# Storing the high and low parts of a matmul's moving operand in alternating pieces of 32 tokens

## The chip, the cores and the metric

The kernel runs on one core of a Trainium2 chip. The metric is the device time of one launch in microseconds. 256 columns are 256 tokens throughout.

## The reference

Two transformer blocks work on 256 latent tokens of 1024 channels. The first block normalizes and modulates the tokens, projects them, mixes them (window attention with a sink beside a two-way mLSTM), projects again and applies a SwiGLU. The second block (with 16 meta tokens ahead, 272 in all) has a SwiGLU, a mixer of attention and gated linear attention with a gate per branch, and a second SwiGLU. What matters here is the dense part, nearly all of the work:

```python
def swiglu(h, w_in, w_out):
    gate, up = jnp.split(h @ w_in, 2, axis=-1)
    return (jax.nn.silu(gate) * up) @ w_out
```

Everything is float32. There are three such SwiGLUs, with an inner width of 2816, and between them the input, output, branch and gate projections.

## The kernel before

Activations lie with channels on the 128 partitions and tokens along the free axis, so a dense layer is a chain of matmuls whose stationary operand is a 128x128 block of weights and whose moving operand is one channel block (k) of all tokens. To keep float32 accuracy on the fp32r path, weights and activations are both split into a high and a low part, and every product is three matmuls into one PSUM bank: high weights by high tokens, high weights by low tokens, low weights by high tokens (`split_mm`, L2003 to L2007; the same three, written out, at L2398 for the first output projection).

Weights stream through a ring of four slots: SP's queue loads `raw`, ScalarE copies it to `hi` (L621), VectorE makes `lo` as raw minus hi (L1143), TensorE multiplies. Each matmul has a weight load of its own, which the trace shows as an instruction of its own (PEld).

The token operands are kept in three pairs of buffers:

- `mixH` and `mixL`, [128, 8, 256] each, one behind the other. They hold the mixed tokens of the first block (L2398), the two branches of the second mixer (`branch_part`), and the normalized input of the last SwiGLU (`gu2`).
- `g_high` and `g_low`, the inner activations of the SwiGLUs, read by `down_half`; 256 tokens wide in `dn0` and `dn2`, 272 wide in `dn1`.
- `n_high` and `n_low`, the normalized tokens of all other dense stages, 258, 272 or 256 columns wide. The change leaves them alone.

The stages follow each other in this order on TensorE: input projections, attention and mLSTM, `wout`, `gu0`, `dn0`, `gu1`, `dn1`, `in2k`, `in2g` with the second mixer in between, `brb`, `bra`, `wout2`, `gu2`, `dn2`. `gu` is the gate and up projection, `dn` the down projection. The order is written out by hand; nothing in it depends on a planner. The first stages of `stage`, a buffer for parts of the modulation's weights that GpSimd's queue loads, share their memory with `mixH` and `mixL`.

Of the kernel before, what the change touches and what calls it, by code (L numbers as in the profile page):

```python
# [28 lines left out]
SLOT = HALF * P  # L29
RING = 4  # L30
# [84 lines left out]
def program(nc, dr, out):  # L115
    with ExitStack() as root:
# [27 lines left out]
        mixH = sbuf(root, "mixH", [P, KD, T], F32R)  # L144
        mixL = sbuf(root, "mixL", [P, KD, T], F32R)
# [224 lines left out]
        def inner(store, width):  # L370

            return store[:, 0:KH * width].rearrange("p (k t) -> p k t", k=KH)
# [132 lines left out]
        def _(pool):  # L505
# [12 lines left out]
            def stage_half(n, freed=0):  # L518
# [87 lines left out]
        def _(act):  # L606
# [193 lines left out]
            def heads_out(n, hp):  # L800
# [4 lines left out]
                act.activation(mixH[:, hp, :], head_bank(n), ACT.Copy).then_inc(oh_ready, 1)  # L805
# [98 lines left out]
            for h in range(4):  # L904
# [3 lines left out]
                act.activation(mixH[:, 4 + h, :], HT_BANK[h], ACT.Copy,  # L908
# [16 lines left out]
            def gate_up_shifted(name, ahead):  # L925
                def evac(i, j):
# [6 lines left out]
                    if j == 3:  # L933

                        act.wait_ge(hb_ready, i + 1)
                        act.activation(inner(g_high, T)[:, ds(2 * i, 2), :], hbuf[:, :, 0:T], ACT.Copy).then_inc(gh_ready, 1)
                pipeline(name, 1024, evac, ahead, silu=True, behind=((0,), (1,), (), (2, 3)), shifted=True)

            def gate_up_scaled(name, f, width, ahead):
                def evac(i, j):  # L940
# [4 lines left out]
                    if j == 3:  # L945

                        act.wait_ge(acc_free[1], USE[name] + i + 1)
                        act.activation(inner(g_high, width)[:, ds(2 * i, 2), :], hbuf[:, :, 0:width], ACT.Copy).then_inc(gh_ready, 1)
# [5 lines left out]
            def upper(scale, k, width, t0, updated, to=nH):  # L954

                act.wait_ge(*updated)
                act.activation(to[:, k, 0:width], R[:, k, t0:t0 + width], ACT.Copy, scale=scale).then_inc(nh_ready, 1)
# [124 lines left out]
            for n in range(8):  # L1082
# [11 lines left out]
                if n in LINEAR_AT:  # L1094
                    i = LINEAR_AT[n]
                    act.wait_ge(yb_ready, i + 1)
                    act.activation(mixH[:, 4 + i:8:2, :], og[:, 2 * i:2 * i + 2, 0:T], ACT.Copy).then_inc(ybh_ready, 1)
# [32 lines left out]
        def _(dve):  # L1130
# [57 lines left out]
            def col(c):  # L1188
                return vec[:, c:c + 1]
# [120 lines left out]
            def modulation(n):  # L1310
# [4 lines left out]
                for b in range(2):  # L1315
                    m, w = 16 + 2 * n + b, stage[:, 2 * b + 1 - side, :]
# [105 lines left out]
            def heads_lower(n, hp):  # L1422

                dve.wait_ge(oh_ready, n + 1)
                dve.tensor_tensor(mixL[:, hp, :], head_bank(n), mixH[:, hp, :].bitcast(F32),
# [151 lines left out]
            for h in range(4):  # L1577
                dve.wait_ge(mlh_ready, h + 1 if h < 2 else 4)
                dve.scalar_tensor_tensor(out=mixL[:, 4 + h, :], in0=HT_BANK[h], scalar=col(V_GML + h),
                                         in1=mixH[:, 4 + h, :].bitcast(F32), op0=ALU.mult, op1=ALU.subtract).then_inc(mll_ready, 1)  # L1580
# [63 lines left out]
            def scaled_lower(first, k, width, t0, scale, to=(nH, nL)):  # L1644

                dve.wait_ge(nh_ready, first + k + 1)
                dve.scalar_tensor_tensor(out=to[1][:, k, 0:width], in0=R[:, k, t0:t0 + width],
# [1147 lines left out]
```

## Time and profile before

| | |
|---|---|
| Median of 3 runs | 971.9 us (969.46 to 973.7) |
| The profiled execution's own time | 973.39 us, its span 971.6 us |
| TensorE busy | 956.6 us, 98% of the span |
| Weight loads busy | 888.0 us, 91% |
| VectorE, ScalarE, GpSimd busy | 641.1, 495.0, 66.6 us |
| Mean granted TensorE clock | 0.994 |

A matmul's duration in the trace (some 280 ns at 256 columns) is longer than the step from one matmul's start to the next one's, since they are pipelined. What the stream costs is the step. It is read from a row that gives the first and last start of the matmuls of one source line: with n matmuls on that line, and two of the other two lines between each two, the step is (last start minus first start) / (3 (n - 1)).

### The profile page before, as it was taken

The page shows a single profiled execution, that of the slowest core. Times are in us where ns is not written, and L with a number is a line of the kernel's source. Part 1 is how long each engine was busy: PE and PEld are TensorE (multiplying, and loading weights), DVE is VectorE, ACT ScalarE, POOL GpSimd, SP SyncE. Part 2 cuts the span into 40 slices and gives each one's busy share as a digit, 9 for nine tenths or more (in the row PEclk, how much of TensorE's full clock was granted, in tenths as well). Part 3 has the DMA queues.
Part 4 walks back from the last instruction along what each step waited for, and adds up shares of the span by engine and source line. Part 5 has one row for each costly group of instructions (what it writes and reads, how often), then busy time and mean ns, then how long its engine had stood idle before and what let it go on. Part 6 is the DMA issues. An engine that isn't in the chain of part 4 may idle for free.

```text
span 971.6 us, 19403 instructions
## 1 busy us (share of the span) xinstructions
PE 956.6 (98%) x7543; PEld 888.0 (91%) x7543; DVE 641.1 (66%) x990; ACT 495.0 (51%) x762; POOL 66.6 (7%) x100
## 2 busy tenths in 40 slices
PE   8999999999999999999999999999999999999997
PEld 3776778899999999899999999999999999999997
DVE  4788886687666765765555546665778766665654
ACT  3755647655444544554444434645566555444540
POOL 0012002200000021000000000200210100000000
PEclk9999998999999999999999999999999999999999
DMA  9982447547556696266666844663445566667841
GB/s 346 384 283 88 131 131 231 163 172 216 173 174 182 191 308 177 71 197 173 176 177 183 217 119 129 212 188 108 131 131 173 154 194 204 184 177 220 217 120 43
DMA packets 189183, 176.06 MB, mean 181 GB/s; under 512 B 7312, under 2 KB 177824, under 8 KB 188752
## 3 DMA queue, kind: packets, MB, share of 16 engines
q1 hardware_dynamic: 183456, 154.29, 53.9%
q0 software_dynamic: 4960, 17.64, 5.3%
q10 hardware_dynamic: 720, 3.49, 0.9%
q8 instruction: 31, 0.51, 0.2%
q14 instruction: 16, 0.13, 0.0%
HBM read 174.32 MB, written 1.05 MB: 180 GB/s over the span
## 4 chain that ended last, share of the span: by engine, by line
PE 87%; DVE 8%; ACT 2%; issue 1%; DMA 1%; POOL 0%; DVEq 0%; ACTq 0%; POOLq 0%
PE acc L2005 23%; PE acc L2006 23%; PE acc L2007 23%; PE acc L2398 3%; DVE lo L1143 2%; PE acc L2101 1%; DMA stage<-in_w_late 1%; PE acc L2203 1%; PE acc L2205 1%; PE acc L2204 1%; PE wk L2064 1%; PE wk L2005 1%; PE wk L2006 1%; PE wk L2007 1%; PE wk L2134 1%
## 5 line engine op out<-in xcount | busy, mean ns | idle before, releaser
L1143 DVE TENSOR_TENSOR lo<-raw,hi 128x1024 fp32r<-128x1024 f32 (+1 forms) x259 | 331.5, 1291 | 208.0 <-ACT hi L621 207.7
L621 ACT ACTIVATE hi<-raw 128x1024 fp32r<-128x1024 f32 (+1 forms) x260 | 283.8, 1099 | 133.5 <-PE acc L2007 114.7
L2005 PE MATMUL acc<-n_high,hi 128*128 128x272 f32 (+3 forms) x1016 | 290.5, 286 | 0.5 <-DVE hbuf L1671 0.3
L2006 PE MATMUL acc<-n_low,hi 128*128 128x272 f32 (+3 forms) x1016 | 289.2, 285 | 0.0
L2007 PE MATMUL acc<-n_high,lo 128*128 128x272 f32 (+3 forms) x1016 | 288.1, 284 | 0.0
L2005 PEld LDWEIGHTS acc<-n_high,hi 128*128 128x128 f32 (+1 forms) x1016 | 191.4, 188 | 3.1 <-issue 1.4
L2006 PEld LDWEIGHTS acc<-n_low,hi 128*128 128x128 f32 (+1 forms) x1016 | 191.0, 188 | 0.5
L2007 PEld LDWEIGHTS acc<-n_high,lo 128*128 128x128 f32 (+1 forms) x1016 | 191.0, 188 | 0.2
L2005 PE MATMUL acc<-g_high,hi 128*128 128x256 f32 (+1 forms) x528 | 148.9, 282 | 0.9 <-DVE lo L1143 0.9
L2006 PE MATMUL acc<-g_low,hi 128*128 128x256 f32 (+1 forms) x528 | 149.1, 282 | 0.0
L2007 PE MATMUL acc<-g_high,lo 128*128 128x256 f32 (+1 forms) x528 | 148.7, 282 | 0.0
L2005 PE MATMUL acc<-mixH,hi 128*128 128x256 f32 x400 | 112.9, 282 | 0.5 <-DVE gab L1844 0.4
L2006 PE MATMUL acc<-mixL,hi 128*128 128x256 f32 x400 | 112.1, 280 | 0.0
L2007 PE MATMUL acc<-mixH,lo 128*128 128x256 f32 x400 | 112.1, 280 | 0.0
L2005 PEld LDWEIGHTS acc<-g_high,hi 128*128 128x128 f32 x528 | 99.3, 188 | 1.2 <-DVE lo L1143 1.1
L2007 PEld LDWEIGHTS acc<-g_high,lo 128*128 128x128 f32 x528 | 99.9, 189 | 0.0
L2006 PEld LDWEIGHTS acc<-g_low,hi 128*128 128x128 f32 x528 | 99.1, 188 | 0.0
L2006 PEld LDWEIGHTS acc<-mixL,hi 128*128 128x128 f32 x400 | 76.5, 191 | 0.0
L2005 PEld LDWEIGHTS acc<-mixH,hi 128*128 128x128 f32 x400 | 75.1, 188 | 1.5 <-DVE gab L1844 0.7
L2007 PEld LDWEIGHTS acc<-mixH,lo 128*128 128x128 f32 x400 | 75.1, 188 | 0.0
L566 POOL TENSOR_TENSOR sq<-sq 128x256 f32<-128x256 f32 (+1 forms) x28 | 23.8, 851 | 482.7 <-ACT sq L923 431.0
L923 ACT ACTIVATE sq<-R (+3 forms) x36 | 15.9, 441 | 57.6 <-DVE R L1715 49.9
(424 smaller groups left out, 1254.5 us busy)
## 6 DMA issues: line engine op xcount, KB each, us to landing
raw<-in_w_in SPq DMA_DIRECT2D x52, 512.0 KB, 3.8
raw<-in_w_ffn_in SPq DMA_DIRECT2D x44, 512.0 KB, 3.9
raw<-in_ffn_w_gate SPq DMA_DIRECT2D x44, 512.0 KB, 3.9
raw<-in_ffn_w_up SPq DMA_DIRECT2D x44, 512.0 KB, 3.8
raw<-in_ffn_w_down SPq DMA_DIRECT2D x32, 704.0 KB, 4.8
stage<-in_w_late POOLq DMA_DIRECT2D x24, 512.0 KB, 5.4
raw<-in_w_ffn_out SPq DMA_DIRECT2D x16, 704.0 KB, 6.2
raw<-in_w_out SPq DMA_DIRECT2D x16, 512.0 KB, 3.6
```

Source lines behind the costliest of these rows:

```text
L566: ins = pool.tensor_tensor(sq[:, 0, 0:width], sq[:, 0, 0:width], sq[:, k, 0:width], ALU.add)
L621: act.activation(hi[:, j, 0:width], raw[:, j, 0:width], ACT.Copy).then_inc(hi_ready, 1)
L923: act.activation(sq[:, k, 0:width], R[:, k, t0:t0 + width], ACT.Square).then_inc(sq_ready, 1)
L1143: dve.tensor_tensor(lo[:, j, 0:width], raw[:, j, 0:width], hi[:, j, 0:width].bitcast(F32), ALU.subtract).then_inc(lo_ready, 1)
L2005: pe.matmul(out_, wH, xH, start=start, stop=False)
L2006: pe.matmul(out_, wH, xL, start=False, stop=False)
L2007: return pe.matmul(out_, wL, xH, start=False, stop=stop)
L2064: ins = pe.matmul(SLAB_BANK[n][32 * kk:32 * kk + 32, :], silu_c[:, 4 * q + kk, :], SLAB_MEM[n][2 * q + kk // 2][:, 512 * (kk % 2):512 * (k ...
L2101: pe.matmul(acc[:, 0, 0:width], cink[:, 0, 0, 0:P], cink.rearrange("p a b t -> p (a b t)")[:, 0:width], start=True, stop=True)
L2134: ins = pe.matmul(bank[:, T * m:T * m + T], ws[:, j, w], xs[:, k, 0:T], start=k == 0 and m == 0 and n == 0, stop=k == KD - 1 and n == 2, s ...
L2203: pe.matmul(out_, n5H[:, k, rows], hi[:, k // 2, w], start=k == 0, stop=False)
L2398: ins = pe.matmul(out_, ws[:, j, w], xs[:, k, :], start=k == 0 and m == 0 and n == 0, stop=k == KD - 1 and n == 2, skip_group_check=True)
```

## The change

The two parts of the mixed tokens share one buffer, `mix`, in which 32 tokens of the high part (128 bytes) are followed by the same 32 tokens of the low part, and so on. The two parts of the inner activations do the same in `inner` where the width is 256; at 272, which isn't a multiple of 32, they still lie one behind the other, without the 32 elements of padding that stood between them. So the moving operand of the matmuls that read them has eight pieces of 32 columns with 128 bytes left out between two, and covers 2 KB where it covered 1 KB. ScalarE and VectorE write the same pieces. `stage` takes its slots in another order, so that the same halves of the channel blocks come free at the same time. The order and number of instructions stay as they were on every engine, and so do all other buffers' places.

```diff
-        mixH = sbuf(root, "mixH", [P, KD, T], F32R)
-        mixL = sbuf(root, "mixL", [P, KD, T], F32R)
+        mix = sbuf(root, "mix", [P, KD, T // PIECE, 2, PIECE], F32R)
+        mixH, mixL = mix[:, :, :, 0, :], mix[:, :, :, 1, :]
...
-        g_high = sbuf(ffn2, "g_high", [P, KH * TM], F32R)
+        inner = sbuf(ffn2, "inner", [P, 2 * KH * TM], F32R)
         sbuf(ffn2, "pad_h", [P, 32])
-        g_low = sbuf(ffn2, "g_low", [P, KH * TM], F32R)
...
+        def inner_parts(width):
+
+            if width == T:
+                g = inner[:, 0:2 * KH * T].rearrange("p (k g h c) -> p k g h c", k=KH, h=2, c=PIECE)
+                return g[:, :, :, 0, :], g[:, :, :, 1, :]
+            return tuple(inner[:, n * KH * width:(n + 1) * KH * width].rearrange("p (k t) -> p k t", k=KH) for n in range(2))
...
-                    pool.dma_start(stage[:, 2 * b + 1 - side, :],
+                    pool.dma_start(stage[:, 2 - 2 * side + b, :],
...
-                act.activation(mixH[:, hp, :], head_bank(n), ACT.Copy).then_inc(oh_ready, 1)
+                act.activation(mixH[:, hp], in_pieces(head_bank(n)), ACT.Copy).then_inc(oh_ready, 1)
...
-                        dve.tensor_tensor(inner(g_low, width)[:, ds(2 * i, 2), :], hbuf[:, :, 0:width],
-                                          inner(g_high, width)[:, ds(2 * i, 2), :].bitcast(F32),
+                        high, low = (n[:, ds(2 * i, 2)] for n in inner_parts(width))
+                        dve.tensor_tensor(low, shaped_as(hbuf[:, :, 0:width], low), high.bitcast(F32),
                                           ALU.subtract).then_inc(gl_ready, 1)
...
-            def split_mm(out_, wH, wL, xH, xL, start, stop):
-
+            def split_mm(out_, j, w, xH, xL, start, stop):
+
+                out_, wH, wL = shaped_as(out_, xH), hi[:, j, w], lo[:, j, w]
                 pe.matmul(out_, wH, xH, start=start, stop=False)
                 pe.matmul(out_, wH, xL, start=False, stop=False)
                 return pe.matmul(out_, wL, xH, start=False, stop=stop)
```

## Rows read from the trace of the kernel before

**Rows 1.** The page: busy time of each engine, the granted clock in 40 slices.

```profile
PE 956.6 (98%) x7543; PEld 888.0 (91%) x7543; DVE 641.1 (66%) x990; ACT 495.0 (51%) x762; POOL 66.6 (7%) x100
...
PEclk9999998999999999999999999999999999999999
```

**Rows 2.** The page: the chain that ended last.

```profile
PE 87%; DVE 8%; ACT 2%; issue 1%; DMA 1%; POOL 0%; DVEq 0%; ACTq 0%; POOLq 0%
```

**Rows 3.** TensorE's waits: line waited for, us in total, times, longest.

```profile
PE acc L2101 <- POOL cink L508: 2.5, 1, 2.5
PE wk L2005 <- DVE n_low L1647: 1.7, 4, 0.8
PE acc L2005 <- DVE lo L1143: 0.9, 1, 0.9
```

**Rows 4.** Groups of TensorE by form, of the matmuls that the change touches.

```profile
L2005 PE MATMUL acc<-mixH,hi 128*128 128x256 f32 x400 | 112.9, 282 | 0.5 <-DVE gab L1844 0.4
...
L2005 PE MATMUL acc<-g_high,hi 128*128 128x256 f32 x352 | 98.2, 279 | 0.9 <-DVE lo L1143 0.9
...
L2398 PE MATMUL acc<-mixH,hi 128*128 128x256 f32 x64 | 19.3, 301 | 0.0
...
L2005 PE MATMUL wk<-mixH,hi 128*128 128x256 f32 x16 | 4.4, 276 | 0.0
```

**Rows 5.** Line L2006 in parts of dn0, gu2, dn2: min/median/max ns, first and last start.

```profile
L2006 PEld LDWEIGHTS acc<-g_low,hi x118: 187/188/188, 344.9 to 384.7; 128*128 128x128 f32 x118
L2006 PE MATMUL acc<-g_low,hi x118: 276/276/276, 345.1 to 384.8; 128*128 128x256 f32 x118
...
L2006 PEld LDWEIGHTS acc<-mixL,hi x270: 192/192/192, 799.9 to 895.0; 128*128 128x128 f32 x135
L2006 PE MATMUL acc<-mixL,hi x269: 281/281/281, 800.0 to 894.7; 128*128 128x256 f32 x135
...
L2006 PE MATMUL acc<-g_low,hi x142: 281/281/281, 905.1 to 954.9; 128*128 128x256 f32 x142
```

**Rows 6.** The same line at 258 columns (gu0), 272 columns (gu1) and 272 columns (dn1).

```profile
L2006 PE MATMUL acc<-n_low,hi x238: 277/283/294, 232.1 to 318.0; 128*128 128x258 f32 x119
...
L2006 PE MATMUL acc<-n_low,hi x254: 287/288/296, 429.8 to 524.7; 128*128 128x272 f32 x127
...
L2006 PE MATMUL acc<-g_low,hi x157: 287/291/292, 534.8 to 593.7; 128*128 128x272 f32 x157
```

**Rows 7.** TensorE in order of time around the first pass of gu2.

```profile
782.38 0.28 PE L2005 MATMUL wk<-mixH,hi 128*128 128x256 f32 x1
782.50 0.28 PE L2006 MATMUL wk<-mixL,hi 128*128 128x256 f32 x1
782.61 0.28 PE L2007 MATMUL wk<-mixH,lo 128*128 128x256 f32 x1
782.73 0.59 PE L2051 MATMUL wk<-sq,cst 128*128 128x256 f32 x2
783.16 1.03 PE L2055 MATMUL wk<-sq,cst 128*128 128x256 f32 x4
```

**Rows 8.** Stretches: PE, PEld, DVE, ACT, POOL busy, granted clock, DMA share, GB/s.

```profile
345.00:385.00 40.00, 40.00 (x355) 40.00 (x355) 24.72 (x24) 17.84 (x23) 8.18 (x8) 1.00 0.85 247
800.00:895.00 95.00, 95.00 (x809) 95.00 (x808) 58.22 (x61) 44.94 (x59) 0.00 (x0) 1.00 0.69 199
```

**Rows 9.** ScalarE and VectorE groups that write the two parts.

```profile
L948 ACT ACTIVATE g_high<-hbuf 128x512 f32 x9 | 5.7, 632 | 18.2 <-DVE hbuf L1671 18.2
...
L1674 DVE TENSOR_TENSOR g_low<-hbuf,g_high 128x512 f32 x9 | 6.2, 693 | 8.6 <-ACT g_high L948 8.6
...
L1647 DVE SCALAR_TENSOR_TENSOR mixL<-R,vec,mixH 128x256 fp32r<-128x256 f32 x8 | 4.2, 568 | 1.4 <-ACT mixH L957 1.4
```

More of the change, by code:

```diff
@@ L29 @@
 SLOT = HALF * P
+PIECE = 32
 RING = 4
@@ L368, in keys_to, with in_pieces, shaped_as, pieces @@
             return META + P * (b + 1)
-        def inner(store, width):
-            return store[:, 0:KH * width].rearrange("p (k t) -> p k t", k=KH)
+        def in_pieces(a):
+            return a.rearrange("p (g c) -> p g c" if len(a.shape) == 2 else "p k (g c) -> p k g c", c=PIECE)
+        def shaped_as(a, other):
+            return in_pieces(a) if len(other.shape) > len(a.shape) else a
+        def pieces(s):
+            return slice(s.start // PIECE, s.stop // PIECE)
+        def inner_parts(width):
[3 more added lines that the diff above has]
+            return tuple(inner[:, n * KH * width:(n + 1) * KH * width].rearrange("p (k t) -> p k t", k=KH) for n in range(2))
         def chunk(c):
@@ L947, in evac @@
                         act.wait_ge(acc_free[1], USE[name] + i + 1)
-                        act.activation(inner(g_high, width)[:, ds(2 * i, 2), :], hbuf[:, :, 0:width], ACT.Copy).then_inc(gh_ready, 1)
+                        high = inner_parts(width)[0][:, ds(2 * i, 2)]
+                        act.activation(high, shaped_as(hbuf[:, :, 0:width], high), ACT.Copy).then_inc(gh_ready, 1)
                 pipeline(name, 1024, evac, ahead, silu=True, behind=((0,), (1,), (), (2, 3)))
@@ L1646, in scaled_lower @@
                 dve.wait_ge(nh_ready, first + k + 1)
-                dve.scalar_tensor_tensor(out=to[1][:, k, 0:width], in0=R[:, k, t0:t0 + width],
-                                         scalar=scale, in1=to[0][:, k, 0:width].bitcast(F32),
+                high, low = (n[:, k] if to[0] is mixH else n[:, k, 0:width] for n in to)
+                dve.scalar_tensor_tensor(out=low, in0=shaped_as(R[:, k, t0:t0 + width], low), scalar=scale, in1=high.bitcast(F32),
                                          op0=ALU.mult, op1=ALU.subtract).then_inc(nl_ready, 1)
@@ L1700, in evac @@
                         dve.wait_ge(gh_ready, i + 1)
-                        dve.tensor_tensor(inner(g_low, T)[:, ds(2 * i, 2), :], hbuf[:, :, 0:T],
-                                          inner(g_high, T)[:, ds(2 * i, 2), :].bitcast(F32), ALU.subtract).then_inc(gl_ready, 1)
+                        high, low = (n[:, ds(2 * i, 2)] for n in inner_parts(T))
+                        dve.tensor_tensor(low, in_pieces(hbuf[:, :, 0:T]), high.bitcast(F32), ALU.subtract).then_inc(gl_ready, 1)
                 pipeline(name, 1024, evac, ahead, peel=True, behind=((0,), (), (), (1, 2, 3)), shifted=True)
@@ L2446, in gate_up @@
             def gate_up(name, t0, width, behind, first, steps, operands=(nH, nL)):
-                xs = (lambda k: operands[0][:, k, t0:t0 + width], lambda k: operands[1][:, k, t0:t0 + width])
+                xs = [lambda k, n=n: n[:, k] if n is mixH or n is mixL else n[:, k, t0:t0 + width] for n in operands]
                 g = BASE[name]
@@ L2482, in down_half @@
             def down_half(name, f, width, i, s):
+                high, low = inner_parts(width)
                 set_free(s, USE[name] + i)
@@ L2489, in down_half @@
                         w = slice(P * kk, P * kk + P)
-                        ins = split_mm(acc[:, 2 * s, 0:width], hi[:, j, w], lo[:, j, w], inner(g_high, width)[:, k, :],
-                                       inner(g_low, width)[:, k, :], k == 0, k == KH - 1)
+                        ins = split_mm(acc[:, 2 * s, 0:width], j, w, high[:, k], low[:, k], k == 0, k == KH - 1)
                     ins.then_inc(mm_done, 1)
```

37 lines of the change are left out of this document (19 added, 18 removed).

## The prediction

> **What bounds the kernel now.** I read the page first: TensorE is busy 98% of the span, VectorE 66%, ScalarE 51%, and the granted clock is near full, which is the 2.4 GHz level, in every slice but the seventh [rows 1]. The chain that ended last is TensorE for 87% [rows 2], and TensorE's longest waits are 2.5, 1.7 and 0.9 us in total [rows 3]. So the time is the length of TensorE's stream, and only two things move it: the number of matmuls, which stays, and the step from one matmul's start to the next one's.
>
> Then I read the steps. In dn0, at 256 columns, 118 matmuls of one line start between 345.1 and 384.8 us, so the step is 39.7 / (3 x 117) = 113.1 ns [rows 5]. In gu2 it is 94.7 / (3 x 268) = 117.8 ns, and in dn2 49.8 / (3 x 141) = 117.7 ns [rows 5]. dn0 and dn2 run the same code from the same buffers at the same width, and yet differ by 4.6 ns. Within each stretch nothing varies: the matmuls' durations are 276 ns from minimum to maximum in dn0 and 281 in dn2 and gu2. So the stream has a short step and a long step at the same width and layout, and keeps the one it has.
>
> What puts it there? Not load from elsewhere: the short-step stretch has the busier DMA engines (0.85 against 0.69) and busy time on GpSimd, the long-step one none, both at clock 1.00 [rows 8]. Up to 782.6 us gu2's own first matmuls still have steps of 0.11 to 0.12 us and the 276 ns duration of the short step (the sixteen on wk in [rows 4]); then six matmuls of the sum of squares stand between [rows 7], and after them the rest of gu2 and dn2 has the long step. So the step is picked anew when the stream restarts. With the long step in gu2 the weight load for one of the three matmuls takes 192 ns instead of 188 [rows 5]: weight loads and the moving operand's reads hold each other up, by amounts that hang on how they stand in time and in address. At 256 columns the channel blocks are a multiple of 256 bytes apart, and each matmul meets the weights in the same place as the last one. At 258 and 272 columns the blocks begin 64 bytes further each time, relative to the weights' 512-byte blocks. There durations spread from 277 to 294 and from 287 to 296 ns, and the steps are 85.9 / (3 x 237) = 120.8 and 94.9 / (3 x 253) = 125.0 ns [rows 6].
>
> **The change part by part.**
>
> Matmuls touched: 400, 352, 64 and 16 groups of three [rows 4], 2,496 matmuls. The ones with the long step are gu2 without its first 48, 1,056 - 48 = 1,008, and dn2's 528: 1,536. The other 960 (the first wout, dn0, the branches, gu2's first) are taken to have the short one. What they cost now is 960 x 113.1 + 1,536 x 117.8 ns = 108.6 + 180.9 = 289.5 us.
>
> The moving operand in pieces: no matmul of before reads with gaps, so no row prices it. The pieces are 128 bytes long, and each matmul's operand now stays in one half of every 256 bytes: a high part never reads where the low part does. The weight load still walks over all of them. From below: at 2.4 GHz, one column per cycle, 256 columns take 106.7 ns, which no stretch reaches; all 2,496 there would be 266.3 us, 23.2 less. From above: the layouts that are out of step with the weights, cut to 256 columns. 120.8 less two columns is 120.0; 125.0 less sixteen columns (6.7) is 118.3. All at 120.0 is 299.5 us, 10.0 more. I take the short step's 113.1, since the blocks keep their distance of whole 256 bytes, with the high part starting at the same place as before relative to the weights: the meeting of the two streams stays regular, and a read that skips half of the lines leaves them free for the weight load for longer at a time. 2,496 x 113.1 = 282.3 us, a gain of 7.2 us. This choice is the least certain of all.
>
> A rule speaks against it. The row shows that a step is 4.6 ns longer with the same operands, and a weight load 4 ns [rows 5]. The Trainium skill (TensorE: Matmul & The Clock Gate, "Step-by-step: what each phase is for") holds that the moving operand and the weights come over two independent read ports and that loading weights takes no read bandwidth from the running matmul. By it there is nothing to gain from a layout, and the sum would be 0. The trace disagrees at least with its plain form.
>
> The 272-wide inner activations in dn1: the low part moves by 128 bytes against the weights. 528 matmuls with a step of 58.9 / (3 x 156) = 125.9 ns [rows 6], where gu1 at the same width has 125.0. At most about a nanosecond either way, 0.5 us; I take 0.
>
> ScalarE and VectorE write and read in pieces: 632 and 693 ns for 512 elements, 568 for 256 [rows 9]. They are engines with a third of the time free, and TensorE's wait for them is short. Only gu2's start waits for them block by block. If pieces cost a quarter more there, eight instructions of 568 ns give 8 x 142 ns = 1.1 us; otherwise other work covers them. From below, nothing. I take 0. Should the cover go, the 22 instructions on 512 elements add at a quarter some 22 x 0.17 = 4 us on each engine, still far from TensorE's load.
>
> The `stage` slots: the same sizes, the same waits, the same channel blocks freed. 0. The PSUM side stays contiguous. 0. What is late next if the stream gets 4% quicker in gu2 and dn2: the weights, split by VectorE, which is at 58.22 of 95 us there [rows 8] and kept up with dn0's short step.
>
> Sum against the profiled execution: 973.4 - 7.2 = 966.2 us. That execution was 1.5 us above the median shown, so against the median 964.7. The other executions may have split into the two steps in another way, so I say 965.5.
>
> **The rivals.** What a measurement of this kernel can tell from no change is about 0.5%, 4.9 us.
>
> *Out of step (slower).* The low part now starts 128 bytes further on against the weights than the high part, so that the three matmuls of a product no longer meet their weight loads in one place, as at 258 and 272 columns. For it: every layout that isn't in step with the weights costs 118.3 to 120.0 ns at 256 columns [rows 6], and that before was in step both for high and low. Against it: those layouts drift from block to block, this one doesn't. At 119.2 ns the sum is 297.5 us, 8.0 more: 980. It decides from a step of 117.9 ns (4.9 us more) up.
>
> *No difference.* The pieces are read like any others, and the stream falls into stretches of either step by its restarts. With the long one throughout it is 2,496 x 117.8 = 294.0, 4.5 more, 976.4; with each where it is now, 972. For it: the step changed without any change of layout [rows 7].
>
> *Nearly free of collisions.* Skipped lines leave the weight load its own lines, and the step falls below 113. Halfway between 113.1 and one column per cycle, at 109.9 ns, the sum is 274.3, 15.2 less: 958 against the profiled execution, 957 against the median. For it: even the short step is 6.4 ns above one column per cycle, so something is left to win. Against it: no stretch at 256 columns shows less, and the weight load still crosses the half in use. The Trainium skill (TensorE: Matmul & The Clock Gate, "Wait — 56ns, not 53.3ns?") gives back-to-back matmuls a fixed cost of about 2.5 ns over the columns; by it the step would be 109.2, the sum 272.6 us and the gain 16.9. No run here shows it.
>
> **How the numbers follow.** Short step throughout 0.36, out of step 0.26, no difference 0.24, nearly free 0.14. Within the first, the gain of 7.2 passes 4.9 us in three of four cases, since the median of before may hold more of the short step than its profile: faster 0.27, same 0.09. Nearly free is all faster: 0.14. No difference: same 0.20, slower 0.04. Out of step passes 4.9 us nearly always: slower 0.23, same 0.03. Together faster 0.41, same 0.32, slower 0.27. The range reaches from the nearly free case, 955, to the out-of-step case's 980; below it lies 0.07, above 0.10. The likeliest case's own range is 962 to 969.
>
> **What would show it right or wrong.** The changed profile shows the same numbers of instructions and no new wait of TensorE. dn0 stays at 113.1 ns and a duration of 276; gu2 and dn2 fall from 117.8 to it, with weight loads at 188 ns. dn1 and gu1 keep their 125.9 and 125.0. Wrong is the step if dn0 rises above 118: then pieces are out of step with the weights. If dn0 falls below 112, they avoid collisions altogether. If dn0 and dn2 still differ, the restarts decide, not the layout. A new wait on `mixL` or `inner` at a stage's start would show that the writes in pieces weren't hidden.

## The result: 0.95% slower, with one step of 120 ns in place of two

The changed kernel takes 979.67 us (median of 4 runs, 979.17 to 980.63), the kernel before 971.46 us beside it (4 runs, 969.46 to 973.7). The ratio is 1.0095, with a 95% interval from 1.0072 to 1.0119: slower by more than the half per cent that this measurement can tell. The two medians by themselves are 8.2 us apart. The profiled execution took 980.06 us, its span 978.3, against 973.39 and 971.6 before. The prediction said 965.5 us and faster. Its range of 955 to 980 holds the median, just.

The page of the changed kernel, with the lines that answer to [rows 1] and [rows 2]:

```profile
PE 962.6 (98%) x7543; PEld 895.8 (92%) x7543; DVE 640.4 (65%) x990; ACT 495.0 (51%) x762; POOL 68.9 (7%) x100
...
PEclk9999999999999999999999999999999999999999
...
PE 88%; DVE 6%; ACT 2%; DMA 2%; issue 1%; SPq 1%; DVEq 0%; ACTq 0%
```

TensorE has the same 7,543 matmuls and is busy 6.0 us longer. VectorE and ScalarE have the same instructions and, within 0.7 us, the same load. The granted clock is near full, the 2.4 GHz level, in all slices; a stretch at the lower level that is too short for the slices to show comes up below. TensorE's longest waits, as in [rows 3] (line waited for, us in total, times, longest):

```profile
PE acc L2119 <- POOL cink L523: 2.5, 1, 2.5
PE wk L2023 <- DVE n_low L1665: 1.7, 4, 0.8
PE wk L2082 <- DMA raw<-in_w_ada: 0.9, 2, 0.6
```

No wait is new. What is left is the step. Line L2006 of before is L2024 now. The rows give the duration (min/median/max, ns) and the first and last start, for part of dn0, gu2, all of dn2, then gu0 (258 columns), gu1 and dn1 (272 columns), as in [rows 5, 6], and last `wout2`, an untouched layout at 256 columns:

```profile
L2024 PEld LDWEIGHTS acc<-inner,hi x112: 187/189/190, 344.8 to 384.8; 128*128 128x128 f32 x112
L2024 PE MATMUL acc<-inner,hi x112: 281/282/282, 344.9 to 384.9; 128*128 128x256 f32 x112
...
L2024 PE MATMUL acc<-mix,hi x265: 281/281/282, 799.7 to 894.8; 128*128 128x256 f32 x133
L2024 PEld LDWEIGHTS acc<-mix,hi x264: 187/189/190, 800.0 to 894.7; 128*128 128x128 f32 x132
...
L2024 PE MATMUL acc<-inner,hi x176: 281/282/283, 905.6 to 968.6; 128*128 128x256 f32 x176
...
L2024 PE MATMUL acc<-n_low,hi x238: 277/283/294, 232.0 to 318.0; 128*128 128x258 f32 x119
...
L2024 PE MATMUL acc<-n_low,hi x255: 287/288/296, 429.7 to 525.0; 128*128 128x272 f32 x128
...
L2024 PE MATMUL acc<-inner,hi x159: 286/288/289, 534.7 to 593.9; 128*128 128x272 f32 x159
...
L2024 PE MATMUL acc<-n_low,hi x41: 276/281/283, 757.8 to 771.9; 128*128 128x256 f32 x41
```

- dn0: 40.0 / (3 x 111) = 120.1 ns, where it was 113.1 [rows 5].
- gu2: 95.1 / (3 x 264) = 120.1 ns, where it was 117.8; dn2: 63.0 / (3 x 175) = 120.0, where it was 117.7 [rows 5].
- gu0 and gu1, whose layout stays, are at 86.0 / (3 x 237) = 121.0 and 95.3 / (3 x 254) = 125.1, within 0.2 ns of [rows 6]. dn1 is at 59.2 / (3 x 158) = 124.9, one nanosecond below its 125.9 [rows 6].

So the three touched stretches at 256 columns now have one and the same step, 120.0 ns, longer than either of the two that before had. The weight load hints at a cause other than that of the old long step: there one of three took 192 ns [rows 5], here it takes 189. Nor is the new stream regular. In order of time in dn2 (start, duration), successive matmuls start 0.13, 0.11 and 0.12 us apart. The trace's own nanoseconds have six steps that come back over and over, 125, 116, 120, 117, 122 and 120, where in dn2 of the kernel before all lie between 117 and 119:

```profile
919.76 0.29 PE L2025 MATMUL acc<-inner,lo 128*128 128x256 f32 x1
919.89 0.28 PE L2023 MATMUL acc<-inner,hi 128*128 128x256 f32 x1
920.00 0.28 PE L2024 MATMUL acc<-inner,hi 128*128 128x256 f32 x1
920.12 0.28 PE L2025 MATMUL acc<-inner,lo 128*128 128x256 f32 x1
920.24 0.28 PE L2023 MATMUL acc<-inner,hi 128*128 128x256 f32 x1
```

The profile gives back the whole difference. The first starts of line L2006 or L2024 in each stage say where it arises (us):

| from | before | after | gained or lost |
|---|---|---|---|
| start to gu0's first product | 199.8 | 199.1 | -0.7 |
| first to last of dn0 | 329.2 to 389.9 | 328.5 to 392.5 | +3.3 |
| last of dn0 to `brb` | to 725.6 | to 727.6 | -0.6 |
| `brb`, `bra`, `wout2`, to gu2 | to 774.5 | to 777.6 | +1.1 |
| gu2, to dn2 | to 900.0 | to 905.6 | +2.5 |
| first to last of dn2 | to 962.0 | to 968.6 | +1.0 |

Together +6.6 of the 6.7 us between the two profiled executions. The third row holds dn1's gain, 0.5 us.

The first row hides a loss. The first wout (64 of the 480 groups of [rows 4] on the mixed tokens) takes 39.0 us from its first start to its last in both kernels, other matmuls in between included. Yet its step went up. The third line of its threes, in its last 96 matmuls, before and after:

```profile
L2398 PE MATMUL acc<-mixH,lo x32: 276/276/281, 181.3 to 191.9; 128*128 128x256 f32 x32
...
L2416 PE MATMUL acc<-mix,lo x32: 281/283/287, 180.0 to 191.2; 128*128 128x256 f32 x32
```

That is 10.6 / (3 x 31) = 114.0 and 11.2 / (3 x 31) = 120.4 ns, 0.6 us for these 96. All but the first 24 matmuls lie in three stretches, 19.1 us together before and 20.1 after: 1.0 us. What makes up for it is TensorE's clock. The stretch from 150 to 160 us, before and after (columns as in [rows 8]), and two of the first 24 matmuls of each kernel:

```profile
150.00:160.00 10.00, 10.00 (x56) 8.38 (x50) 7.86 (x23) 9.01 (x17) 2.82 (x4) 0.66 0.86 298
...
150.00:160.00 10.00, 10.00 (x64) 8.44 (x60) 9.62 (x29) 9.02 (x16) 2.82 (x4) 0.83 0.88 307
...
154.12 0.41 PE L2398 MATMUL acc<-mixH,lo 128*128 128x256 f32 x1
154.34 0.41 PE L2398 MATMUL acc<-mixH,hi 128*128 128x256 f32 x1
...
154.09 0.41 PE L2416 MATMUL acc<-mix,hi 128*128 128x256 f32 x1
154.30 0.41 PE L2416 MATMUL acc<-mix,lo 128*128 128x256 f32 x1
```

Behind the mLSTM's matmuls, with TensorE busy all of the time from 140 us on in both, the granted clock falls to 0.50, the 1.2 GHz level: for 6.8 us before, for 3.4 us after (twice the 0.34 and the 0.17 of 10 us that the row has it below full). So the profiled execution of before lost 1.7 us more to the clock than that of after. The profiled executions of the next two experiments, pieces of 64 and the moved low part, have a granted clock of 1.00 in this stretch, and the four later ones of whole kernels 0.83, so its length varies by itself. Without it the two profiles would be some 6.7 + 1.7 = 8.4 us apart (an estimate), close to the medians' 8.2.

The same matmuls show something else. At the 1.2 GHz level the step is 213 ns with the pieces (some 16 matmuls) and without (24). The change costs nothing there; the loss shows at 2.4 GHz only.

`wout2`'s own step went up too, with its layout as it was: its median duration was 276 ns and is 281, the sign of the long step. A step is picked at a restart, and the stages ahead of it had changed. How often chance alone would pick the other one isn't known: one execution of each kernel was profiled.

The groups of ScalarE and VectorE that write the pieces, as in [rows 9]:

```profile
L964 ACT ACTIVATE inner<-hbuf 128x512 f32 x9 | 5.7, 632 | 18.2 <-DVE hbuf L1688 18.2
...
L1692 DVE TENSOR_TENSOR inner<-hbuf,inner 128x512 f32 x9 | 6.2, 693 | 9.4 <-ACT inner L964 9.4
...
L1665 DVE SCALAR_TENSOR_TENSOR mix<-R,vec,mix 128x256 fp32r<-128x256 f32 x8 | 4.2, 568 | 1.4 <-ACT mix L974 1.4
```

632, 693 and 568 ns, to the nanosecond what they were. For these operations, reading and writing in pieces of 128 bytes costs nothing.

### The profile page after: what moved, and what is told of

Its sections match the earlier page's. It is cut to its first block, busy times and chain, and to the rows that moved or that the text cites. A ratio compares the mean times of both kernels' runs of the same rounds, so it can differ in the third digit from the quotient of the medians.

```text
span 978.3 us, 19430 instructions
## 1 busy us (share of the span) xinstructions
PE 962.6 (98%) x7543; PEld 895.8 (92%) x7543; DVE 640.4 (65%) x990; ACT 495.0 (51%) x762; POOL 68.9 (7%) x100
## 4 chain that ended last, share of the span: by engine, by line
PE 88%; DVE 6%; ACT 2%; DMA 2%; issue 1%; SPq 1%; DVEq 0%; ACTq 0%
PE acc L2023 24%; PE acc L2025 24%; PE acc L2024 24%; PE acc L2416 3%; DMA slab_hi<-in_w_ada 1%; PE acc L2221 1%; PE acc L2223 1%; PE acc L2222 1%; DVE lo L1160 1%; PE wk L2023 1%; PE wk L2025 1%; PE wk L2024 1%; DMA crow<-in_crow 1%; PE wk L2716 1%; PE acc L2152 1%
## 5 line engine op out<-in xcount | busy, mean ns | idle before, releaser
L2024 PE MATMUL acc<-n_low,hi 128*128 128x272 f32 (+3 forms) x1016 | 289.4, 285 | 0.0
L2024 PEld LDWEIGHTS acc<-n_low,hi 128*128 128x128 f32 (+1 forms) x1016 | 191.0, 188 | 0.5
L2023 PE MATMUL acc<-inner,hi 128*128 128x256 f32 (+1 forms) x528 | 150.1, 284 | 0.7 <-DVE lo L1160 0.7
L2025 PE MATMUL acc<-inner,lo 128*128 128x256 f32 (+1 forms) x528 | 150.4, 285 | 0.0
L2024 PE MATMUL acc<-inner,hi 128*128 128x256 f32 (+1 forms) x528 | 149.8, 284 | 0.0
L2023 PE MATMUL acc<-mix,hi 128*128 128x256 f32 x400 | 113.5, 284 | 0.4 <-DVE gab L1861 0.4
L2025 PE MATMUL acc<-mix,lo 128*128 128x256 f32 x400 | 113.6, 284 | 0.0
L2024 PE MATMUL acc<-mix,hi 128*128 128x256 f32 x400 | 112.6, 282 | 0.0
L2023 PEld LDWEIGHTS acc<-inner,hi 128*128 128x128 f32 x528 | 99.2, 188 | 0.9 <-DVE lo L1160 0.9
L2024 PEld LDWEIGHTS acc<-inner,hi 128*128 128x128 f32 x528 | 99.5, 189 | 0.0
L2025 PEld LDWEIGHTS acc<-inner,lo 128*128 128x128 f32 x528 | 99.2, 188 | 0.0
L2023 PEld LDWEIGHTS acc<-mix,hi 128*128 128x128 f32 x400 | 75.1, 188 | 1.2 <-DVE gab L1861 0.6
L2024 PEld LDWEIGHTS acc<-mix,hi 128*128 128x128 f32 x400 | 75.5, 189 | 0.0
L2025 PEld LDWEIGHTS acc<-mix,lo 128*128 128x128 f32 x400 | 75.2, 188 | 0.0
```

Of the source, the lines that this page charges most:

```text
L2023: pe.matmul(out_, wH, xH, start=start, stop=False)
L2024: pe.matmul(out_, wH, xL, start=False, stop=False)
L2025: return pe.matmul(out_, wL, xH, start=False, stop=stop)
```

## The experiments

In before and after the weights `hi` and `lo` begin 160 bytes past a multiple of 256 and the mixed and inner tokens of before at 96, so that the tokens stand 192 bytes past the weights, modulo 256. "Place" means this distance below. After keeps the high pieces at place 192 and has the low ones at 64. Two things changed for TensorE: the operand is read in pieces of 128 bytes with gaps, and the low part stands elsewhere.

### Pieces of 64 tokens, by turns

```diff
-PIECE = 32
+PIECE = 64
```

> The change with pieces of 64 tokens instead of 32, so a piece is 256 bytes. Read in order, high and low part then touch the same places within 256 bytes as before the change, and both start at the same one; only the gaps stay (three in a matmul instead of seven). Theory 1 (the step depends on where the two reads stand within 256 bytes, gaps cost nothing): dn0 back at a step of 113.1 or 117.8 ns, time within 3 us of 971.5. Theory 2 (each gap costs about 1 ns, seven made 120.0 out of 113.1): dn0 and dn2 both at 116 ns, time about 972 as well, since gu2 and dn2 were at 117.8. The steps tell them apart, the time doesn't. Theory 3 (any pattern with gaps is slower by a fixed amount): 120 ns, 980 us.

Measured: 970.56 us against 970.19 of the kernel before (12 and 21 runs), ratio 1.0004 (0.9989 to 1.0019). Line L2024 in parts of dn0, gu2 and dn2:

```profile
L2024 PE MATMUL acc<-inner,hi x104: 276/276/276, 344.9 to 379.9; 128*128 128x256 f32 x104
...
L2024 PE MATMUL acc<-mix,hi x256: 281/281/281, 799.8 to 889.9; 128*128 128x256 f32 x128
...
L2024 PE MATMUL acc<-inner,hi x128: 281/281/281, 904.9 to 949.8; 128*128 128x256 f32 x128
```

35.0 / (3 x 103) = 113.3, 90.1 / (3 x 255) = 117.8 and 44.9 / (3 x 127) = 117.8 ns: the steps of before, in the same stages. With pieces of 256 bytes the low part is at the high part's place, and gaps as such, high and low by turns and all the writing in pieces are free. What is left are the size of the piece and the low part's other place.

### Only the low part 128 bytes further, no pieces

The kernel before, with a buffer moved between the parts:

```diff
+        rsum = sbuf(root, "rsum", [P, 32])
         mixL = sbuf(root, "mixL", [P, KD, T], F32R)
...
-        rsum = sbuf(root, "rsum", [P, 32])
...
         g_high = sbuf(ffn2, "g_high", [P, KH * TM], F32R)
-        sbuf(ffn2, "pad_h", [P, 32])
         g_low = sbuf(ffn2, "g_low", [P, KH * TM], F32R)
+        sbuf(ffn2, "pad_h", [P, 32])
```

> No pieces and no gaps: the layout of before, but the low part of the mixed tokens and of the inner activations begins 128 bytes further on within 256 bytes than the high part, as it does in the change. Theory 1a (the low part's other place against the weights makes the long step): dn0, gu2 and dn2 at about 120 ns, time 978 to 981 us. Theory 2 (the gaps do it): dn0 at 113.1 ns and time as before, 971.5. In between (the place of each part within 256 bytes matters, and so does that a part stays in one half): a step other than 113.1, 117.8 and 120.0.

Measured: 975.29 us against 970.19, ratio 1.0055 (1.0036 to 1.0074). The line of high weights by low tokens, in the same three stages:

```profile
L2007 PE MATMUL acc<-g_low,hi x99: 282/282/283, 345.1 to 379.7; 128*128 128x256 f32 x99
...
L2007 PE MATMUL acc<-mixL,hi x256: 282/282/283, 799.8 to 889.9; 128*128 128x256 f32 x128
...
L2007 PE MATMUL acc<-g_low,hi x128: 282/282/283, 904.8 to 949.7; 128*128 128x256 f32 x128
```

34.6 / (3 x 98) = 117.7 ns, then 117.8 and 117.8. The "out of step" rival's mechanism is real but smaller than its size: it takes the short step away in all three stretches and gives the long one. It doesn't give 120. The "about 120" expected by that theory missed, so something else in the pieces has to bring the rest.

### Only the mixed tokens in pieces

The inner activations as before, the mixed tokens as after:

```diff
-        mixH = sbuf(root, "mixH", [P, KD, T], F32R)
-        mixL = sbuf(root, "mixL", [P, KD, T], F32R)
+        mix = sbuf(root, "mix", [P, KD, T // PIECE, 2, PIECE], F32R)
+        mixH, mixL = mix[:, :, :, 0, :], mix[:, :, :, 1, :]
```

> Only the mixed tokens in pieces of 32 by turns; the inner activations lie as before the change. Both theories: the 1,440 matmuls on mixed tokens at 120.0 ns; dn0 stays at 113.1 ns; dn2 at one of its two steps, 113.1 or 117.8. Of the change's 8.2 us, 432 x 6.9 ns + 1,008 x 2.2 ns = 5.2 us stay with dn2 at 117.8, 2.7 us with dn2 at 113.1: 974 to 977 us. If the writes in pieces by ScalarE and VectorE were what costs, a new wait of TensorE would show on the mixed tokens, and the steps would be as before.

Measured: 973.85 us against 970.19, ratio 1.0046 (1.0028 to 1.0064), 3.7 us more: between the 2.7 and the 5.2 us that were expected, if just below the 974 us named. Parts of dn0, gu2 and dn2:

```profile
L2022 PE MATMUL acc<-inner,lo x104: 276/276/276, 344.8 to 379.8; 128*128 128x256 f32 x104
...
L2022 PE MATMUL acc<-mix,lo x250: 281/284/287, 800.1 to 889.7; 128*128 128x256 f32 x125
...
L2022 PE MATMUL acc<-inner,lo x133: 276/276/281, 904.7 to 949.8; 128*128 128x256 f32 x133
```

gu2 has 89.6 / (3 x 249) = 119.9 ns. dn0 stays at 113.3, and dn2 has 45.1 / (3 x 132) = 113.9 over this stretch where the kernel before had 117.7. dn2's code, buffers and places are as before; only what runs ahead of it differs. That fits a restart that picks the other step, in the other direction this time; with one profiled execution of each kernel, what ran ahead and chance can't be told apart here.

### The layout alone, measured by itself

A kernel of nothing but such threes (it leaves out the rest of the reference), called the bench below: 17 layouts, each with 8 starts of 48 matmuls; a first matmul of 128 to 142 columns shifts the start. Its core, where `part` returns the token operand at a place and in pieces:

```python
pe.matmul(acc[:, 1, 0:128 + 2 * t], hi[:, 0:128], x[:, 0:128 + 2 * t], start=True, stop=True)
...
pe.matmul(o, hi[:, w], h, start=g == 0, stop=False)
pe.matmul(o, hi[:, w], l, start=False, stop=False)
pe.matmul(o, lo[:, w], h, start=False, stop=g == 15)
```

> TensorE alone on resident data: 48 matmuls of 256 columns in the kernel's pattern (high weights by high, high weights by low, low weights by high, channel blocks 1 KB apart), for 17 layouts, each started 8 times with a different number of columns ahead. The output is not the reference's: only one product block is computed. Flat layouts start 0 to 224 bytes past the weights within 256 bytes, in steps of 32. Theory 1: the step is a function of the place within 256 bytes and of the start; at 192 bytes 113.1 or 117.8 ns by the start, other places 117 to 121; with the low part 128 bytes off (flat192_64) about 120; turns of 64 and 128 tokens at 192 bytes the same two values as flat; turns of 32 at 192 bytes 120.0 whatever the start; turns of 16 unlike flat. Theory 2 (gaps): flat with the low part off at 113 or 118, turns of 128, 64, 32, 16 at 114, 116, 120, 128; gaps of 32 with both parts at the same place 120.

One row for each layout gives the last matmul of every three, from the first to the last of its 384 matmuls: contiguous at place 0, contiguous at 192 (before), low part 128 bytes further (the second experiment), pieces of 32 by turns at 192 (after), and pieces of 32 with gaps but high and low at the same place:

```profile
L73 PE MATMUL acc<-x,lo x128: 280/283/287, 23.2 to 69.6; 128*128 128x256 f32 x128
...
L127 PE MATMUL acc<-x,lo x128: 276/281/283, 301.6 to 346.9; 128*128 128x256 f32 x128
...
L145 PE MATMUL acc<-x,lo x128: 279/280/281, 393.7 to 439.3; 128*128 128x256 f32 x128
...
L181 PE MATMUL acc<-x,lo x128: 281/282/287, 580.9 to 627.4; 128*128 128x256 f32 x128
...
L217 PE MATMUL acc<-x,lo x128: 282/283/284, 766.0 to 812.5; 128*128 128x256 f32 x128
```

From first to last that is 46.4, 45.3, 45.6, 46.5 and 46.5 us. The steps below are the mean over the last 24 matmuls of each start, from their starts in the trace, without the shifting matmuls:

| layout | step, ns |
|---|---|
| contiguous, place 0; 96 | 120.0 |
| contiguous, 32 | 116.7, once 117.8 |
| contiguous, 64; 128; 224 | 117.8; 118.5; 118.3 |
| contiguous, 160 | 117.2 to 118.8 |
| contiguous, 192 (before) | 113.3 in 2 of 8 starts, 117.8 in 6 |
| contiguous, high 192, low 64 | 117.8 in all 8 |
| pieces of 32 by turns, at 0; 64; 192 | 120.0 in all 8 |
| pieces of 32 by turns, at 128 | 120.0 to 121.1 |
| pieces of 16 by turns, at 192 | 120.7 |
| pieces of 64 by turns; of 128 by turns | 113.3 in 3 of 8, else 117.8 |
| pieces of 32 with gaps, high and low both at 192 | 120.0 in all 8 |

This settles it. The last line has the pieces of after without their low part's other place, and has 120.0 all the same. Pieces of 128 bytes or less are the cause, at any of the places tried; the other place is no part of it. Three things come together in them, though, and no run takes them apart: the length of a piece, that each operand stays in one half of every 256 bytes, and the shape of the instruction, which reads and writes in runs of 32 (or 16) elements. Contiguous place 0 has 120.0 too, but with every step at 120 ns, without the pattern of pieces by turns. And the bench has before's two steps with nothing else running: no other engine, no DMA beside it, only another start.

### More places, and two parts at different ones

> The same bench as for the first set of layouts, all flat, TensorE alone: places between the ones already measured (16, 48, ... 240 bytes past the weights within 256 bytes), and the high part at 192 bytes with the low part at 200, 208, 224, 0, 32, 96, 128 or 160. The output is not the reference's. If the step is a smooth function of the place, the odd places fall between their neighbours (116.7 to 120). If reads come in units of 32 bytes, a place of 16 bytes more behaves like the one below it or like none. With parts at different places no layout should keep 113.3 from all starts; the theory that the short step needs both parts in one place says that none of the eight mixed ones reaches 113.3 at all.

Contiguous again, 8 starts each, the same reckoning: 16 gave mostly 118.7, but 113.3 from one start and 116.8 from another; 48 118.3, 80 120.0 (once 118.3), 144 118.7 in five and 116.7 in three, 176 119.2, 208 119.2 (once 116.7), 240 117.1 ns. Place 112 gave 113.3 from all 8 starts, far below its neighbours 96 and 128, so the step is no smooth function of the place. Its last matmuls take 275 ns, and the whole lasts 44.3 us where contiguous 192 had 45.3:

```profile
L100 PE MATMUL acc<-x,lo x128: 275/275/282, 161.7 to 206.0; 128*128 128x256 f32 x128
```

With the high part at 192 and the low part at another of eight places (200, 208, 224, 0, 32, 96, 128, 160), steps lay between 116.9 and 120.0; none reached 113.3. With the high part at 192 no other place of the low part had the short step.

### A wider matmul now and then

Contiguous at 192, in rounds of 24 matmuls; the first of each round is 0, 2, 4 ... 14 columns wider.

> The bench with the flat layout at 192 bytes, eight starts each, in rounds of 24 matmuls whose first one is 0, 2, ... 14 columns wider (the extra columns go to unused PSUM columns). The output is not the reference's. Theory: the step that a stream settles into is set by where in a period of a few cycles a matmul starts, so that the widening moves the long step's pattern on and, for some width, into the short step, which then stays. For 0 extra columns 2 or 3 of 8 starts are at 113.3 in all rounds and the others at 117.8; for at least one width all or nearly all starts end at 113.3 but for the widened matmul. Rival: a widening is a new start each time, so that every round falls to short or long with the same odds, and no width does better than the mean of some 116.5 ns.

Rows of the last matmul of each three over 8 starts of 120 matmuls, for no wider matmul and for six columns more:

```profile
L80 PE MATMUL acc<-x,lo x320: 276/281/283, 21.3 to 133.8; 128*128 128x256 f32 x160
...
L95 PE MATMUL acc<-x,lo x320: 276/276/281, 358.6 to 468.3; 128*128 128x256 f32 x160
```

Without it two of eight starts keep 113.3 and six keep 117.8 for all 120 matmuls. With 2, 8, 10, 12 or 14 columns more the rounds alternate between a short and a long step; with 4, one short round follows two long ones. With six, all eight starts are at 113.3 from the second round on, and the whole takes 109.7 us where it was 112.5, though it issues more columns. In the short stream the step behind a widened matmul is 116 to 117 ns, some 3 ns more, and 113.3 follows. So six columns lead out of the long step, and from the short one back into the short one. That it is the shift in time that does it fits the trace and isn't shown.

### 258 and 272 columns

> The bench at 258 and 272 columns with channel blocks 1,088 bytes apart, which move 64 bytes on each time, so that only the place within 64 bytes is free: 0, 16, 32 and 48 bytes past the weights, each block used twice (gate and up) or once (down), eight starts each. The output is not the reference's. Theory: place 0 gives the means of the kernel, 120.9 (258), 125.0 (272, twice) and about 125.9 (272, once); the other three differ from it by up to 2 ns either way, since a good and a bad place average out over four blocks.

Channel blocks 1088 bytes apart, places modulo 64. The rows for 258 columns at place 0 and 16:

```profile
L79 PE MATMUL acc<-x,lo x192: 278/283/289, 22.3 to 92.4; 128*128 128x258 f32 x192
...
L84 PE MATMUL acc<-x,lo x192: 277/281/287, 92.9 to 162.1; 128*128 128x258 f32 x192
```

By steps: 120.8, 119.2, 120.8 and 119.0 to 119.4 ns at places 0, 16, 32 and 48. At 272 columns the four places give 124.6 to 125.3 with each block used twice (gu), and 125.0 to 126.1 with each used once (dn). So dn1's single nanosecond is of the size that a place makes, and 16 bytes are worth up to 1.7 ns at 258 columns.

### Place 112 in the kernel, by moving the weights

The kernel before, with the weights 80 bytes further:

```diff
-        hi = sbuf(root, "hi", [P, RING, SLOT], F32R)
-        lo = sbuf(root, "lo", [P, RING, SLOT], F32R)
+        wts = sbuf(root, "wts", [P, 2 * RING * SLOT + 8], F32R)
+        hi, lo = (wts[:, 4 + n * RING * SLOT:4 + (n + 1) * RING * SLOT].rearrange("p (j w) -> p j w", j=RING) for n in range(2))
```

> The layout of before, flat, but both weight buffers begin 80 bytes further on within 256 bytes, so that the 256-column operands stand 112 bytes past the weights instead of 192. On the bench that place gave 113.3 ns from all eight starts. Theory (the step is set by the place, the start picks only where two steps exist): dn0, gu2, dn2, the branches and the first output projection all at 113.3 ns; 1,536 matmuls 4.5 ns shorter, 6.9 us less than before, 964, up to 6 us more or less for the 258- and 272-column stages, whose place moves too. Rival (the real kernel's other engines or its restarts push the stream out of the short step): dn2 or gu2 at more than 115 ns and no gain.

Measured: 983.34 us against 971.96, ratio 1.0119 (1.0093 to 1.0146), slower than after. Parts of dn0 and gu2:

```profile
L2006 PE MATMUL acc<-g_low,wts x98: 284/285/285, 345.0 to 379.9; 128*128 128x256 f32 x98
...
L2006 PE MATMUL acc<-mixL,wts x254: 279/280/284, 800.0 to 889.8; 128*128 128x256 f32 x127
```

34.9 / (3 x 97) = 119.9 and 89.8 / (3 x 253) = 118.3 ns, not 113.3. The distance between the operands was that of the bench and the step was not. In the bench the weights stood on a multiple of 32 bytes and the tokens 16 off one; here it is the other way round. The theory that the distance decides by itself fell. And dn0 and gu2 differ by 1.6 ns here, at one width and one place: the order in which blocks are used counts too, or the weights' own blocks. The bench has gu2's order only, each block of tokens twice in a row, and none of its steps at 256 columns was measured in dn0's.

### The wider matmul in the kernel

In gu2, dn0 and dn2 of the kernel before the first matmul of every 48 or 66 is six columns wider; the extra columns go into a part of PSUM that nothing reads.

```diff
-                pe.matmul(out_, wH, xH, start=start, stop=False)
+                pe.matmul(*((wide[0], wH, wide[1]) if wide else (out_, wH, xH)), start=start, stop=False)
```

> The layout of before; in the loops of gu2, dn0 and dn2 the first of every 48 or 66 matmuls is six columns wider (the extra columns are written behind the tokens in PSUM and not read). On the bench six more columns led all eight starts into the short step within two rounds. Theory: gu2 and dn2 fall to 113.3 ns after the first passes, for 2.5 ns per widened matmul: 6 to 7 us less than before, 964 to 966. Rival: in the kernel the waits at the start of each pass set the start anew, and the steps stay as before: 971.

Measured: 965.47 us against 971.96, ratio 0.9931 (0.9908 to 0.9953). gu2 and dn2:

```profile
L2006 PE MATMUL acc<-mixL,hi x265: 276/276/279, 799.9 to 889.8; 128*128 128x256 f32 x133
...
L2006 PE MATMUL acc<-g_low,hi x133: 276/276/279, 905.0 to 949.9; 128*128 128x256 f32 x133
```

89.9 / (3 x 264) = 113.5 and 44.9 / (3 x 132) = 113.4 ns. The layout is that of before, to the byte, and the long step is gone from these loops. It is not gone from the kernel: in this execution `wout2` and the first groups of gu2, which have no wider matmul, had it (medians of 281 ns, steps of 117.8), where the kernel before had the short one.

### Place 112 by moving the tokens

The weights on a multiple of 32 bytes, the tokens of all three pairs 16 bytes off one and 112 past the weights, everything contiguous. The core of the edit, in the kernel before:

```diff
-        mixH = sbuf(root, "mixH", [P, KD, T], F32R)
-        mixL = sbuf(root, "mixL", [P, KD, T], F32R)
+        mix = sbuf(root, "mix", [P, 2 * KD * T + 8], F32R)
+        mixH, mixL = (mix[:, 4 + n * KD * T:4 + (n + 1) * KD * T].rearrange("p (k t) -> p k t", k=KD) for n in range(2))
...
-        g_low = sbuf(ffn2, "g_low", [P, KH * TM], F32R)
+        sbuf(ffn2, "pad_h", [P, 24])
+        g_low = sbuf(ffn2, "g_low", [P, KH * TM + 8], F32R)[:, 4:KH * TM + 4]
```

> As the last try with place 112, but now, as on the bench, the weights begin on a multiple of 32 bytes and the token operands 16 bytes off one (for the 256-column stages of all three pairs of buffers); there it was the other way round. Flat layout. Theory (both the distance and each operand's own place within 32 bytes count; the bench's 113.3 ns from all starts needs the weights on the multiple): dn0, gu2, dn2, the second output projection and the branches at 113.3 ns, 258 columns at 119.5 instead of 120.8 ns as on the bench at place 48, 272 in dn1 at 125.5: 6.9 + 1.4 us less than before, 962 to 965. Rival (what made place 112 fail is the kernel's restarts or its other engines, not the 32-byte place): dn0 at 118 to 120 ns again and 975 to 985 us.

Measured: 963.78 us (961.91 to 965.47) against 972.37, ratio 0.991 (0.9893 to 0.9927). It beats both kernels. dn0, gu2, dn2, and gu0 at 258 columns:

```profile
L2008 PE MATMUL acc<-g_high,lo x104: 275/275/275, 344.8 to 379.8; 128*128 128x256 f32 x104
...
L2008 PE MATMUL acc<-mix,lo x265: 275/275/275, 800.0 to 889.8; 128*128 128x256 f32 x133
...
L2008 PE MATMUL acc<-g_high,lo x133: 275/275/275, 905.1 to 949.9; 128*128 128x256 f32 x133
...
L2008 PE MATMUL acc<-n_high,lo x241: 277/282/287, 232.1 to 317.9; 128*128 128x258 f32 x121
```

113.3, 89.8 / (3 x 264) = 113.4 and 44.8 / (3 x 132) = 113.1 ns, with durations of 275 ns without spread in all three stages: in this execution no restart falls into the long step. gu0 has 85.8 / (3 x 240) = 119.2, the bench's value for 16 bytes further, where before had 120.8 [rows 6].

## Why the prediction was wrong

The step that failed is this one: "I take the short step's 113.1, since the blocks keep their distance of whole 256 bytes, with the high part starting at the same place as before relative to the weights: the meeting of the two streams stays regular, and a read that skips half of the lines leaves them free for the weight load for longer at a time." Measured is 120.0 ns in dn0, gu2 and dn2 and some 120 in the first wout, and the experiments deny both halves of the reason. Pieces of 32 at the same place as before still have 120.0, so the place of a piece's start doesn't carry the step over. Leaving lines free bought nothing with pieces of 64 tokens (1.0004) and went with 6.9 ns more with pieces of 32. The term was 2,496 x 113.1 = 282.3 us; it is 2,496 x 120.0 = 299.5, 10.0 over the 289.5 of before and not 7.2 under. The two profiles show 3.3 us of it in dn0, 2.5 in gu2, 1.0 in dn2, 1.1 around the branches and `wout2`, and 1.0 in the first wout, 8.9 in all; dn1 gives 0.5 back. The medians differ by 8.2.

The other steps:

- *TensorE's stream bounds the kernel, and only the step can move it.* Right: same count of instructions, no new wait, and the stages' positions add up to 6.6 of 6.7 us. Left out was the clock: the short stretch at 1.2 GHz moves the time of one execution by up to an estimated 3.4 us, half of 6.8.
- *One layout has two steps, and restarts choose.* Right, and shown: the bench has both from one layout by its start alone, and the wider matmul takes the long one away without a byte moved. The count of matmuls with the long step was 24 too high, worth 0.1 us: the trace has the short step in gu2's first 72 and not in its first 48. Shown wrong is what I made of it: that pieces would pick the shorter of the two. They have a third step, 120.0, from all eight starts.
- *The bound from above, 120.0 ns*, worked out from the layouts with another pitch [rows 6], is what came, and with it the end of the range. The trace couldn't tell that this was the value to take. I set the odds by how regular the meeting of the streams would be, and regular turned out to be no sign of short: 120.0 is the bench's value for contiguous place 0, just as regular.
- *"Out of step"* had the right side and nearly the right size, 980 us by 119.2 ns, and the wrong mechanism. The low part 128 bytes further makes 117.8 and 1.0055. After's 120.0 needs no such offset.
- *Writers in pieces cost nothing, dn1 at most a nanosecond:* right: 632, 693 and 568 ns unchanged, dn1 124.9 for 125.9.
- *What would show it wrong:* "Wrong is the step if dn0 rises above 118" came true; the conclusion set beside it, that pieces are then out of step with the weights, didn't hold as meant.

The sum itself was sound. 2,496 matmuls at the short step gave a gain of 7.2 us; the wider matmul, which has that step in dn0, gu2 and dn2, gained 6.5 (965.47 for 971.96), and the tokens at place 112 gained 8.6 (963.78 for 972.37), with a share of its own from gu0. The gain was there, and another edit gets it.

The rule weighed against the trace has its answer too. The layouts of the bench differ in nothing but where the operands lie and in what pieces, and their steps run from 113.3 to 121.1 ns. The Trainium skill (TensorE: Matmul & The Clock Gate, "Step-by-step: what each phase is for") says that weights are loaded over a read port of their own and take no read bandwidth from the running matmul. Taken plainly that makes the change worth 0, and the runs disagree with this conclusion: with one weight load per matmul, place decides over 6%. They don't disagree with the two ports, since no run shows that the weight load is the other party. The Trainium skill (TensorE: Matmul & The Clock Gate, "Wait — 56ns, not 53.3ns?") has a fixed 2.5 ns over the columns, which would be 109.2 ns, an estimate; no stretch at 256 columns of any run here came below 113.1.

Open is the physical cause: what it is in the memory or in TensorE's reads that 128-byte pieces, the place modulo 256 and 16 bytes within 32 run into, and why 1.2 GHz hides it (213 ns in both kernels). That it is a collision with the weight load is argued from its dependence on the distance to the weights; no kernel here ran the same threes without their weight loads. Open too is whether pieces of 128 bytes hurt by their length or because each operand stays in one half of every 256 bytes: pieces of 64 bytes, which don't stay in one half, had 120.7, but no layout had 128-byte pieces in alternating halves. And none read contiguous tokens with an instruction in runs of 32, so its shape is a rival that stands untested.

## What to carry to other kernels

When TensorE is bound by its stream, read the step from the first and last start in each stage, and treat two steps at one width as a sign that the addresses of weights and tokens, and the stream's restarts, matter (here 4% of the step between short and long). Check the granted clock around each stage before you compare two profiles: here it was worth 1.7 us between them, a quarter of their difference. Try places first in a kernel of nothing but these matmuls, in the order of each stage and with several starts, try the best again in the whole kernel, and choose a layout that has the short step from every start: here tokens 112 bytes past the weights, weights on a multiple of 32 bytes, worth 0.9%. Keep a moving operand contiguous over at least 256 bytes (the smallest piece that cost nothing here), and don't argue a gap to be helpful because it leaves memory free.

## What the runs showed that I had not expected

- A three-matmul product at 256 columns with one weight load each has steps from 113.3 to 120.0 ns by the tokens' place relative to the weights modulo 256, in places by the start as well.
- At place 192 two steps, 113.3 and 117.8, each kept for 120 matmuls on end; the start chooses. Six extra columns in one matmul lead from the long one to the short one, the other six widths tried lead out of the short one again.
- The step hangs on each operand's own address and not on the distance only: 112 bytes apart gave 113.3 with the weights on a multiple of 32 bytes, and 118.3 to 119.9 with the weights 16 bytes off one and the tokens on one.
- Pieces of 64 tokens with gaps are free for TensorE, pieces of 32 cost 2.2 to 6.7 ns a matmul, and ScalarE and VectorE don't notice pieces of 32 (632, 693 and 568 ns unchanged).
- At the 1.2 GHz level 256 columns take 213 ns with pieces and without; all of the difference arises at 2.4 GHz.
